# Eight gate and value blocks of each pointwise feed-forward stage as seven quarter products over tokens

## The reference

```
def swiglu(h, w_gate_up, w_down):
    a, b = jnp.split(h @ w_gate_up, 2, axis=-1)
    return (jax.nn.silu(a) * b) @ w_down

x = x + 0.5 * swiglu(rms_norm(x, norm), w_gate_up, w_down)   # 1024 -> 2 x 2816 -> 1024
```

## Time and profile before

| | |
|---|---|
| three runs | 1436.49, 1436.63, 1436.96 us (median 1436.63) |
| span of the profiled execution | 1434.9 us; the three runs lie 1.6 to 2.1 us above it |
| PE, DVE, ACT, POOL busy in the span | 1429.6, 985.0, 802.0, 144.3 us |
| granted TensorE clock | 1.00 in every stretch |
| one block of a pointwise stage, PE | 8.29 us |
| weight tiles loaded | 486 of 512 KB, 3.5 us median from issue to landing |

### The profile page before, as it was taken

How to read it: one execution, slowest core, us unless ns; L and a number is a source line. 1 busy time by engine, 2 the same in 40 slices (tenths; PEclk the granted TensorE clock), 3 DMA queues, 4 the chain that set the end, 5 groups by cost and what they waited for, 6 DMA issues and landing times.

```text
span 1434.9 us, 20812 instructions
## 1 busy us (share of the span) xinstructions
PE 1429.6 (100%) x8064; PEld 1232.8 (86%) x8064; DVE 985.0 (69%) x1602; ACT 802.0 (56%) x1409; POOL 144.3 (10%) x211
## 2 busy tenths in 40 slices
PE   9999999999999999999999999999999999999999
PEld 7888888898888888888888898888888899888887
DVE  7656676777666566666676677665676977778776
ACT  6545556754555555455566746554557765455553
POOL 0100024000000001000050004000038300100000
PEclk9999999999999999999999999999999999999999
DMA  8655565354655547555564455556546335446551
GB/s 340 245 194 188 190 205 191 133 187 162 223 189 186 198 139 242 191 191 190 176 234 138 157 190 202 181 190 197 196 156 233 130 122 184 162 169 220 194 187 59
DMA packets 73681, 267.76 MB, mean 187 GB/s; under 512 B 8176, under 2 KB 8304, under 8 KB 73456
## 3 DMA queue, kind: packets, MB, share of 16 engines
q1 hardware_dynamic: 73296, 265.65, 55.3%
q10 hardware_dynamic: 288, 0.79, 0.1%
HBM read 265.36 MB, written 1.05 MB: 186 GB/s over the span
## 4 chain that ended last, share of the span: by engine, by line
PE 100%; DVE 0%; issue 0%; POOL 0%; POOLq 0%
PE bank L559 30%; PE bank L566 15%; PE bank L513 9%; PE bank L514 9%; PE bank L515 8%; PE bank L580 4%; PE bank L585 4%; PE bank L581 4%; PE bank L543 3%; PE bank L550 3%; PE bank L544 3%; PE bank L533 1%; PE bank L748 1%; PE bank L759 1%; PE bank L774 1%; PE bank L806 1%
## 5 line engine op out<-in xcount | busy, mean ns | idle before, releaser
L1630 DVE TENSOR_TENSOR wlo<-raw,whi 128x1024 fp32r<-128x1024 f32 (+1 forms) x481 | 579.7, 1228 | 14.4 <-ACT whi L1097 14.4
L1097 ACT ACTIVATE whi<-raw 128x1024 fp32r<-128x1024 f32 (+1 forms) x481 | 490.0, 1048 | 5.1 <-DMA raw<-w_dram 2.4
L559 PE MATMUL bank<-hx,whi 128*128 128x512 f32 x1856 | 452.4, 392 | 0.0
L559 PEld LDWEIGHTS bank<-hx,whi 128*128 128x128 f32 x1856 | 343.7, 188 | 71.1 <-issue 3.0
L566 PEld LDWEIGHTS bank<-hx,wlo 128*128 128x128 f32 x1856 | 241.9, 191 | 11.7
L566 PE MATMUL bank<-hx,wlo 128*128 128x256 f32 x1856 | 245.5, 282 | 0.0
L513 PE MATMUL bank<-whi,hid 128*128 128x512 f32 x536 | 211.2, 394 | 0.0
L514 PE MATMUL bank<-wlo,hid 128*128 128x512 f32 x536 | 209.9, 392 | 0.0
L515 PE MATMUL bank<-whi,hid 128*128 128x512 f32 x536 | 208.6, 389 | 0.0
L1726 DVE TENSOR_TENSOR sil<-sil,bank 128x256 f32<-128x256 f32 x80 | 33.6, 420 | 182.1 <-ACT sil L1186 182.1
L1186 ACT ACTIVATE sil<-bank 128x256 f32<-128x256 f32 x80 | 30.6, 383 | 211.5 <-PE bank L566 211.5
(11 more groups left out here) (257 smaller groups left out, 1536.8 us busy)
## 6 DMA issues: line engine op xcount, KB each, us to landing
raw<-w_dram SPq DMA_DIRECT2D x486, 512.0 KB, 3.5
gain<-g_dram SPq DMA_DIRECT2D x7, 512.0 KB, 3.8
arena<-c_dram SPq DMA_DIRECT2D x2, 768.0 KB, 6.8
cst<-c_dram SPq DMA_DIRECT2D x1, 1056.0 KB, 5.9
out_dram<-x SPq DMA_DIRECT2D x4, 256.0 KB, 2.0
par<-p_dram SPq DMA_DIRECT2D x1, 867.0 KB, 7.6
raw<-w_dram SPq DMA_DIRECT2D x2, 432.0 KB, 3.1
gain<-g_dram ACTq DMA_DIRECT2D x1, 512.0 KB, 5.0
```

What stands on the lines that cost most here:

```text
L559: e.matmul(b[:, :], hi_of(j)[:, k * P:k * P + P], hx[:, k * 2 * S:k * 2 * S + 2 * S], start=k == 0, stop=False, skip_group_check=True)
L1097: e.activation(hi_of(t), raw_of(t), ACT.Copy).then_inc(sem["w_hi"], 1)
L1630: e.tensor_tensor(lo_of(t), raw_of(t), hi_of(t).bitcast(F32), ALU.subtract).then_inc(sem["w_lo"], 1)
```

## The change

In the four pointwise stages, feature blocks 11 to 14 and 18 to 21 no longer have `a` and `b` tiles. Each group of four (512 gate columns and 512 value columns) is computed by tokens. The input is cut into quarters by token half and by half of the 1024 features (X11, X12, X21, X22), the weights into quarters by feature half and gate or value (11, 12, 21, 22), and instead of eight quarter products there are seven:

| n | input | weights | buffer |
|---|---|---|---|
| 0 | X11 | 11 | G, loaded |
| 1 | X12, added into the bank of 0 | 21 | streamed as before |
| 2 | X12 + X21 - X22 - X11 | 22 | H, loaded |
| 3 | X11 - X21 | 22+12 | H, first addition |
| 4 | X21 - X22 - X11 | 22+12+11 | H, second addition |
| 5 | X21 - X22 | 11+12 | G, addition |
| 6 | X22, added into the bank of 3 | all four | H, third addition |

Every product has two tiles (h = 0, 1), each of 6 matmuls of 512 columns. The weight sums are made by transfers that add into SBUF, issued by POOL (`add_forms`): each waits until DVE has split the buffer's present content (`w_lo`), and ACT's rounding of the new form waits for its landing. G and H lie in `gates`, which the mixers use otherwise; SP loads their first forms (`load_form`). The four input forms are made once per stage: DVE sums high and low input (two of 128x1024) and makes four combinations of 128x512 in block 2, ACT rounds 128x2048 in block 3, DVE subtracts 128x2048 in block 4. The products stand behind the `accum` of the blocks that `SLOTS` names. Their results are combined on ACT and DVE (`chunk`: four ACT operations and seven DVE operations of 128x512 per group), and `turn_chunk` turns them back to features with two lots of four transposes, at i = 11 and 12, and 18 and 19. In those blocks PE does only the transposes, `accum` and the product, and ACT and DVE split the hidden block straight from the bank; the claim of `turn` is released by `hidlo` of its second block. Banks for products 0 and 3 leave the ring until product 1 and 6. The tiles that enter ACT's and DVE's split grow by 6 per group.

```
+GROUPS = (11, 18)
+SLOTS = {3: ((0, 0),), 4: ((0, 1),), 5: ((0, 2),), 6: ((0, 3),), 7: ((0, 4),), 8: ((0, 5),), 9: ((0, 6),),
+         10: ((1, 0),), 11: ((1, 1),), 12: ((1, 2),), 13: ((1, 3),), 15: ((1, 4), (1, 5)), 16: ((1, 6),)}
+CHUNK = {o + q: (c, q) for c, o in enumerate(GROUPS) for q in range(4)}
+NORMAL = [i for i in range(2, NF) if i not in CHUNK]
...
+FORMS = (("G", 0), (None, 0), ("H", 0), ("H", 1), ("H", 2), ("G", 1), ("H", 3))
+ADDED = {("G", 0): "11", ("G", 1): "12", ("H", 0): "22", ("H", 1): "12", ("H", 2): "11", ("H", 3): "21"}
+PER = {"G": 2, "H": 4}
...
+        def gated(tag, st, i):
+            for c, k in SLOTS.get(i, ()):
+                cc = self.chunk_no(tag, c)
+                if k == 0:
+                    held[c, 0] = claim((tag, "s", c, 0), "sil", 2 * cc + 1, True)
+                if k == 1:
+                    ring.append(held[c, 0])
+                if k == 2:
+                    claim((tag, "s", c, 2), "tokv", cc + 1)
+                if k == 3:
+                    held[c, 3] = claim((tag, "s", c, 3), "comb", 5 * cc + 5, True)
+                if k in (4, 5):
+                    claim((tag, "s", c, k), "comb", 5 * cc + k - 3)
+                if k == 6:
+                    ring.append(held[c, 3])
...
+            def product(s, c, n):
+
+                tag = STAGES[s]
+                cc = K.chunk_no(tag, c)
+                b = claim((tag, "s", c, {1: 0, 6: 3}.get(n, n)))
+                if n == 1:
+                    E.wait_ge("tokp", cc + 1)
+                if n == 6:
...
+                for h in range(2):
+                    j = T[f"{tag}s{c}{n}{h}"]
+                    half = lambda buf, k: buf[:, (k - 2 * h) * 512:(k - 2 * h) * 512 + 512]
+                    E.wait_ge("w_hi", SI[j] + 1)
+                    for k in (2 * h, 2 * h + 1):
+                        e.matmul(b[:, :], sh(k), half(hi_of(j), k), start=k == 0 and n not in (1, 6), stop=False, skip_group_check=True)
+                        e.matmul(b[:, :], sl(k), half(hi_of(j), k), start=False, stop=False, skip_group_check=True)
+                    E.wait_ge("w_lo", SI[j] + 1)
+                    for k in (2 * h, 2 * h + 1):
+                        ins = e.matmul(b[:, :], sh(k), half(lo_of(j), k), start=False, stop=k == 3, skip_group_check=True)
+                    ins.then_inc(sem["tile"], 1)
...
+                for i in range(2, NF - 1):
+                    if i in CHUNK:
+                        c, q = CHUNK[i]
+                        if q < 2:
+                            turn_chunk(s, c, q)
+                        accum(s, i - 3)
...
+                    for c, n in SLOTS.get(i, ()):
+                        product(s, c, n)
...
+                    if i in CHUNK:
+                        c, q = CHUNK[i]
+                        while due:
+                            chunk(*due.pop(0))
+                        if i == NF - 1:
+                            hi_upto(T[f"{tag}d{i}"])
+                        E.wait_ge("turn", 2 * K.chunk_no(tag, c) + q // 2 + 1)
+                        if q % 2:
+                            E.wait_ge("hidlo", K.HID0[s] + i)
+                        hidden_hi(K.HID0[s] + i, bank[K.BANK[tag, "turn", c, q // 2][0]][:, q % 2 * S:q % 2 * S + S])
...
+                    if i == 3:
+                        input_forms()
+                    if 3 <= i < NF - 1:
+                        ahead(T[f"{tag}d{i - 3}"])
+                    for c, n in SLOTS.get(i, ()):
+                        while due:
+                            chunk(*due.pop(0))
+                        ahead(T[f"{tag}s{c}{n}0"])
+                        ahead(T[f"{tag}s{c}{n}1"])
+                        due.append((c, n))
...
+                def input_forms():
+                    n = 6 * GATED.index(tag)
+                    a11, a12, a21, a22 = (xf[:, i * 512:i * 512 + 512] for i in range(4))
+                    E.wait_ge("xf", n + 2)
+                    e.tensor_tensor(a22, a21, a22, ALU.subtract).then_inc(sem["xf"], 1)
+                    e.tensor_tensor(a21, a11, a21, ALU.subtract).then_inc(sem["xf"], 1)
+                    E.wait_ge("xf", n + 4)
+                    e.tensor_tensor(a11, a22, a11, ALU.subtract).then_inc(sem["xf"], 1)
+                    E.wait_ge("xf", n + 5)
+                    e.tensor_tensor(a12, a12, a11, ALU.add).then_inc(sem["xf"], 1)
...
+                def chunk(c, n):
+
+                    cc = K.chunk_no(tag, c)
+                    if n >= 4:
+                        E.wait_ge("tile", DONE[f"{tag}s{c}{n}1"])
+                        b = bank[K.BANK[tag, "s", c, {6: 3}.get(n, n)][0]]
+                    if n == 4:
+                        E.wait_ge("tokp", cc + 1)
+                        e.tensor_tensor(tokU, tokU, b[:, :], ALU.add).then_inc(sem["comb"], 1)
+                    if n == 5:
+                        E.wait_ge("comb", 5 * cc + 1)
+                        E.wait_ge("turn", 2 * cc)
+                        e.tensor_tensor(tokW, b[:, :], tokU, ALU.subtract).then_inc(sem["comb"], 1)
+                        E.wait_ge("comb", 5 * cc + 2)
+                        E.wait_ge("tokv", cc + 1)
+                        e.tensor_tensor(tokV, tokV, tokW, ALU.add).then_inc(sem["comb"], 1)
+                        e.tensor_tensor(tokW, tokW, bank[K.BANK[tag, "s", c, 3][0]][:, :], ALU.subtract).then_inc(sem["comb"], 1)
+                        E.wait_ge("comb", 5 * cc + 3)
+                        E.wait_ge("sil", 2 * cc + 1)
+                        e.tensor_tensor(tokS, tokS, tokV, ALU.mult).then_inc(sem["tokm"], 1)
+                    if n == 6:
+                        e.tensor_tensor(tokU, tokU, b[:, :], ALU.add).then_inc(sem["comb"], 1)
+                        E.wait_ge("comb", 5 * cc + 4)
+                        E.wait_ge("sil", 2 * cc + 2)
+                        e.tensor_tensor(tokW, tokU, tokW, ALU.mult).then_inc(sem["tokm"], 2)
...
+            def add_forms(s):
+
+                tag = STAGES[s]
+                for c in range(len(GROUPS)):
+                    cc = K.chunk_no(tag, c)
+                    for n in (5, 3, 4, 6):
+                        buf, k = FORMS[n]
+                        before = FORMS.index((buf, k - 1))
+                        for h in range(2):
+                            off = addends[tag, c, ADDED[buf, k], h]
+                            E.wait_ge("w_lo", SI[T[f"{tag}s{c}{before}{h}"]] + 1)
+                            e.dma_start(form[buf][:, h * TW:h * TW + TW], wstream[off * P:(off + TW) * P].rearrange("(p n) -> p n", p=P),
+                                        accum_op=ALU.add).then_inc(sem[f"add_{buf}{h}"], 16)
```

More of the change, by code:

```diff
@@ L1 @@
 import math
+from collections import deque
 from contextlib import ExitStack
@@ L491, in sp_program @@
                 load_tile(j)
+                for tag, c, buf in forms.get(j, ()):
+                    load_form(tag, c, buf)
                 if j == 1:
@@ L731, in ffn @@
                     wide_block(jb, claim((tag, "b", i)))
-                    if i == 2 and not pointwise:
+                    if i == 2:
                         t = claim((tag, "ft", 1))
@@ new lines, in gated, with ffn, low @@
+                finish(s)
+            def ffn(s):
+                tag = STAGES[s]
+                norm_hi(s, 1)
+                t0 = T[f"{tag}p0"]
+                hi_upto(t0 + 5)
+                e.activation(small[:, 12:13], mhalf[:, 0:1], ACT.Gelu)
+                for a in range(2):
+                    E.wait_ge("tok", K.TOK[f"{tag}p"]) if a == 0 else E.wait_ge("tile", K.TOKTILE[f"{tag}p"])
+                    b = bank[K.BANK[f"{tag}p", a][0]]
+                    tb = tokbuf[:, a * 512:a * 512 + 512]
+                    e.activation(tb, b[:, :], ACT.Copy).then_inc(sem["tok_a"], 1)
+                def low(i, part):
+                    E.wait_ge("tile", DONE[f"{tag}{'ab'[part]}{i}"])
+                    m = K.MUL0[s] + i
@@ L1742, in ffn @@
                     ahead(ja)
-                    if i == 2 and pointwise:
-                        t = bank[K.BANK[tag, "ft", 0][0]]
-                        for n in range(2):
-                            hidden_lo(K.HID0[s] + n, t[:, n * S:n * S + S])
                     whole(i, 0)
-                    if not pointwise:
-                        if i == 2:
-                            conv(0)
-                            hidden(0)
-                        else:
-                            if i == 3:
-                                ahead(jb)
-                            conv(i)
+                    if i == 2:
+                        conv(0)
+                        hidden(0)
+                    else:
+                        if i == 3:
+                            ahead(jb)
+                        conv(i)
                     if i < NF - 1:
```

403 lines of the change are left out of this document (313 added, 90 removed).

## The result

The changed kernel takes 1446.07 us (median of 4, 1444.05 to 1447.87) against 1436.79 before: ratio 1.0064, 95% interval 1.0049 to 1.0078. It is slower by 9.3 us where 14.1 us of gain were forecast.

The account below looks back on a forecast made before the run. PE was taken as the bound, 100% of the chain. -17.9 us on PE, +0.4 for input forms, +2.8 for adding transfers and +0.6 for POOL's queue gave -14.1: 1436.6 to 1422.5 us, range 1415 to 1444.

Parts of the forecast that it names:

- the input forms: Blocks 2 to 4 of each pointwise stage: making the four input combinations costs 0.1 us per stage, at most 1.
- The arithmetic of PE and the hidden work: Pointwise stages: seven products and eight transposes replace four blocks' matmuls, gaining 17.9 us; ACT and DVE keep up.
- Rivals 2 and 3: 2: ACT and DVE fall behind, 1426 to 1434 us, chance 0.15; 3: products don't pay on PE, 1433 to 1439, chance 0.05.
- The chain behind the adding transfers: Group 1, blocks 11 to 15: two additions in a row delay block 15's bank; 0.7 us per stage, 2.8 in all.
- X: Time from DVE's release of a form to the landing of the sum; taken as 5.9 us.
- its formula: PE's wait at block 15's bank claim is 2X - 11.1 us per stage, if over zero.
- X = 5.9, nearer to the plain transfer than to the crowded one: Adding transfer's time: 3.3 us median, 1.5 more for reading the destination, 1 for POOL; crowded transfer 7.4.
- Rival 1: Additions too slow: gain gone from X = 7.7 us; with X = 10 the time is 1455 us; chance 0.19.
- The raw buffers smooth that: Blocks 11 to 13: raw buffers absorb a weight stream asking 270 GB/s, 1.4 times the 192 before.
- The page of the Trainium skill: Ratio 1.93 applied to an adding transfer's landing: X would be 6.4 us, the wait 1.7 per stage, 6.8 in all.
- Tables end near 60: L0f1, POOL's queue: additions stand behind the rotary tables, which end near 60 us; cost 0.6 us, once.
- two issues before it just fit: L0f1: X = 5.9 and two issues just fit before product 3 of group 0 starts at about 69.5 us.

Follow-up runs that it names:

- second_half_left_out: tables_between without the addition to the second half of product 3's form in group 1, 4 transfers in all; 1434.23 us, 0.9984 of before.
- tables_between: Changed kernel, but in the first stage GpSimd issues group 0's first four additions before the mixer's tables; 1436.67 us, 0.9998 of before.
- no_additions: tables_between with the 64 adding transfers and the waits for them left out; 1419.76 us, 0.9881 of before.
- product2_at_11: tables_between with product 2 of group 1 behind block 11 instead of block 12; 1438.73 us, 1.0014 of before.

## Why the prediction was wrong, point by point

Forecast and measurement differ by 23.6 us. From the medians: 0.5 us on PE and the input forms, 14.1 us at the additions (16.9 against 2.8), 8.8 us at the tables (9.4 against 0.6). These make 23.4; the rest is the median of before, 1436.8 here and 1436.6 in the forecast.

- **The arithmetic of PE and the hidden work: right.** 17.9 us, less 0.4 for the input forms, were forecast; without the waits 17.0 are there. Products of 2.73 us, 1344 matmuls in each of the two parts, ACT and DVE hidden. The input forms cost 0.4 us, in L1f2 alone, at `accum(1)`. Rivals 2 and 3 are out.
- **The chain behind the adding transfers: right as far as it went, and mis-sized.** The single chain was there, at the claim named, released as named. With the measured landings in place of X its formula comes within 0.5 us in three stages of second_half_left_out, and 0.9 us short in L0f2. Its X is 5.5 to 5.8 us, from release to landing, only for a transfer that is alone in its queue. The step that failed is "X = 5.9, nearer to the plain transfer than to the crowded one": the two halves for product 3 of group 1 go out 1.1 us apart, and the first takes 7.5 to 8.4 us in tables_between, the second 10.3 to 10.6. The forecast knew both halves of a form, and counted the landing of the first.
- **What it left out: the second halves.** They make a second chain, through ACT's order from product 3 to block 15. In the changed kernel PE waits 0.9 to 1.8 us in product 3, 0.66 at `accum(11)` and 1.6 at block 15, in every stage. Rival 1 had the sign; its break-even length was 7.7 us from release to landing, and tables_between, with first halves of 7.8 to 8.7 us by that count, came out at the time of before. That this fits is in part luck: the second of the two additions took only 5.5 to 5.8 us by the same count, so the formula gives 2.2 to 3.4 us a stage, 11.8 in all, and not the 16.9 that were lost.
- **"The raw buffers smooth that": right for the weights, wrong for what it was to excuse.** In no_additions the plain stream makes PE wait nowhere. (48 tiles more on 486 are 10%, not the 9% of the forecast.) But the DMA engines were full for 12 us around the additions, and the forecast reckoned the demand, 270 GB/s, with copied bytes. An added byte holds the engines 1.97 times as long.
- **The page of the Trainium skill.** "Collectives: The Full Stack", section on the bandwidth ceiling, measures collectives among four ranks: one that reduces reaches half the bandwidth of one that copies (ratio 1.93), because each piece needs two source reads. The share of the DMA engines' time in this case agrees, 13.2% against 6.7%. The landings don't stand in that ratio: 7.5 to 5.1 us in the median, and 5.2 to 5.5 against 3.4 to 3.5 for product 4's first half. The forecast had put the ratio on the landing of one transfer.
- **L0f1's tables: right place, wrong size.** "Tables end near 60", and "two issues before it just fit". The constants went out at 47.1, near the forecast, but took 9.9 us to land, and the tables ended at 63.9. Then four additions went out together and the third took 11.6 us. By the forecast's own count (two issues of 1 us, 5.9 to the landing, 1.0 of rounding) these tables alone would make product 3 ready at 72.8, 2.7 us behind PE's 70.1; that is an estimate. The queue that had gathered made it 8.0, and the clock's lower level cost 2.6 more (5.3 us for product 3 and not 2.7).

## What to carry to other kernels

A transfer's price is that of its place in the queue: ask how many go out together, and reckon with the last landing, not the first. Where an engine works in order, a wait for one landing delays all that stands behind it, also what frees a bank or a buffer; a release that two chains end at doesn't move until both do, so leaving one out can show nothing where it matters much. And before an idea is dropped for waits, move its deadline: one product placed one block later, and the tables behind the first additions, turned 9.3 us of loss into 13.9 us of gain.

## What the runs showed of the hardware

- An adding transfer of 512 KB holds the DMA engines 1.97 times as long as a copy (13.2% and 6.7% of the span for the same 9216 packets). Its issue takes GpSimd 0.87 us and the copy's 0.53.
- In a burst on GpSimd's queue each addition landed 2.5 us after the one ahead: 8.0, 9.6, 11.6, 13.5 us after issues 0.5 to 0.8 us apart.
- TensorE's clock fell to its lower level behind short waits in the midst of a busy kernel. In product2_at_11, L1f1, PE stood 3.55 us before 653.14 (windows with the columns of the earlier trace rows):

```profile
650.00:654.00 4.00, 0.86 (x2) 0.77 (x3) 2.56 (x3) 4.00 (x7) 0.88 (x1) 0.77 0.82 139
654.00:660.00 6.00, 6.00 (x17) 4.66 (x17) 5.60 (x8) 4.13 (x5) 0.29 (x1) 0.58 0.99 266
```

In second_half_left_out it did so behind 2.40 us in L1f1, where eight matmuls came 0.43 us apart and cost 1.6 us more, and not behind 2.25 us in L0f2. The length doesn't decide it alone: behind 3.47 us in L0f2 of product2_at_11 the clock stayed up. So a wait of PE can cost more than its length. The kernel in which PE stood 2.4 to 3.6 us in each stage scattered most: product2_at_11 ran from 1433.4 to 1441.8 us, no_additions, which has no such wait, from 1419.6 to 1419.9.
